# Stick-breaking attention: scores, transposes and value products in blocks of a unit, sigmoid written to SBUF, one ring of three PSUM bank pairs

## What is computed

```
z = q . k * scale                       strict: key index < query index
log_beta = log_sigmoid(z)
log_1mb  = where(strict, log_sigmoid(-z), 0)
later    = reverse_cumsum(log_1mb) - log_1mb
a        = where(strict, exp(log_beta + later), 0)
out      = a @ v, then a headwise RMSNorm
```

## Time and profile before

| | us |
|---|---|
| median of 3 runs | 2859.27 |
| profiled execution, its own time | 2860.66 |
| span of the profiled execution | 2858.8 |
| around the span | 1.9 |
| stick-breaking scans, first start | 915.4 |
| last difference, start | 1350.3 |
| first matmul of the output projection | 1364.9 |

### The profile page before, as it was taken

One profiled execution on the slowest core, in us unless ns is written; L12 is line 12 of the kernel. 1 busy time (PEld: TensorE's weight loads), 2 busy tenths in 40 slices (PEclk: granted clock), 3 DMA queues, 4 the chain that ended last, 5 costly groups with the idle time before them and its releaser, 6 DMA issues.

```text
span 2858.8 us, 51825 instructions
## 1 busy us (share of the span) xinstructions
PE 2788.6 (98%) x19192; PEld 2449.8 (86%) x19192; DVE 1894.1 (66%) x2800; ACT 1471.7 (51%) x2572; POOL 861.9 (30%) x947
## 2 busy tenths in 40 slices
PE   7999999999999999999999999999999999999998
PEld 6888778878888877777899999998889998999886
DVE  6214430087777777777577877787478877878656
ACT  5112221177777666666455545554355555655444
POOL 1832222066776786776002221111100000011110
PEclk9999999999999999999999999999999999999999
DMA  5489897466554523520559999999757784899984
GB/s 195 137 191 225 211 231 170 119 156 148 113 133 107 119 60 75 119 82 16 199 164 331 323 284 289 283 285 290 197 165 235 241 252 157 256 328 300 253 230 158
DMA packets 303337, 559.42 MB, mean 196 GB/s; under 512 B 32272, under 2 KB 70160, under 8 KB 301968
## 3 DMA queue, kind: packets, MB, share of 16 engines
q1 hardware_dynamic: 262768, 463.06, 51.0%
q0 software_dynamic: 39072, 92.30, 17.4%
q10 hardware_dynamic: 1312, 1.64, 0.2%
HBM read 449.91 MB, written 197.13 MB: 226 GB/s over the span
## 4 chain that ended last, share of the span: by engine, by line
PE 70%; DVE 4%; DMA 2%; ACT 2%; issue 1%; POOL 1%; SPq 0%; DVEq 0%; ACTq 0%; POOLq 0%
PE f_ps L2507 26%; PE f_ps L2391 19%; PE h_z L714 5%; PE h_o L1003 5%; PE h_z L717 5%; PE h_t L981 4%; PE h_o L939 3%; PE h_t L924 2%; DVE f_wlo L1880 1%; DMA f_wraw<-sums_scratch 1%; PE h_z L716 1%; DVE h_negmax L1178 1%; PE f_ps L2431 0%; PE f_ps L2417 0%; DVE f_xsum L2093 0%
## 5 line engine op out<-in xcount | busy, mean ns | idle before, releaser
L1880 DVE TENSOR_TENSOR f_wlo<-f_wraw,f_whi 128x512 fp32r<-128x512 f32 x834 | 574.7, 690 | 234.1 <-ACT f_whi L1873 232.3
L1873 ACT ACTIVATE f_whi<-f_wraw 128x512 fp32r<-128x512 f32 x834 | 520.8, 627 | 393.8 <-PE f_ps L2507 254.3
L2507 PE MATMUL f_ps<-f_hi_s,f_whi 128*128 128x256 f32 x1408 | 391.2, 278 | 7.1 <-DVE f_up L2232 7.1
L2507 PE MATMUL f_ps<-f_lo_s,f_whi 128*128 128x256 f32 x1408 | 391.7, 278 | 0.0
L2507 PE MATMUL f_ps<-f_hi_s,f_wlo 128*128 128x256 f32 x1408 | 389.8, 277 | 0.0
L1364 POOL TENSOR_TENSOR h_work<-h_more 128x1024 f32<-128x1024 f32 (+7 forms) x192 | 264.7, 1395 | 115.6 <-DVE h_more L1264 115.6
L2507 PE MATMUL f_ps<-f_hi_a,f_whi 128*128 128x256 f32 x1056 | 292.0, 276 | 1.0 <-DVE f_second L2232 1.0
L2507 PE MATMUL f_ps<-f_hi_a,f_wlo 128*128 128x256 f32 x1056 | 291.6, 276 | 0.0
L2507 PE MATMUL f_ps<-f_lo_a,f_whi 128*128 128x256 f32 x1056 | 291.6, 276 | 0.0
L2507 PEld LDWEIGHTS f_ps<-f_hi_s,f_whi 128*128 128x128 f32 x1408 | 264.4, 188 | 8.8 <-DVE f_wlo L1880 4.4
L1264 DVE TENSOR_TENSOR_SCAN h_more<-h_z,h_zero 128x1024 f32<-128x1024 f32 (+7 forms) x128 | 231.7, 1812 | 59.4 <-ACT h_z L1096 56.9
(11 more groups left out here) (203 smaller groups left out, 6448.2 us busy)
## 6 DMA issues: line engine op xcount, KB each, us to landing
f_wraw<-in_w_stream SPq DMA_DIRECT2D x394, 256.0 KB, 4.3
f_wraw<-sums_scratch SPq DMA_DIRECT2D x352, 256.0 KB, 4.8
sums_scratch<-in_w_stream POOLq DMA_DIRECT2D x132, 256.0 KB, 5.4
act_scratch<-f_act SPq DMA_DIRECT2D x88, 256.0 KB, 4.0
combined_acts<-f_act SPq DMA_DIRECT2D x88, 256.0 KB, 5.2
f_wraw<-down_sums SPq DMA_DIRECT2D x88, 256.0 KB, 3.5
f_piece<-combined_acts SPq DMA_DIRECT2D x88, 256.0 KB, 3.1
down_sums<-in_w_stream POOLq DMA_DIRECT2D x66, 256.0 KB, 6.3
```

Source lines behind the costliest of these rows:

```text
L1873: act.activation(w_hi[ring][:], w_raw[ring][:], ACT.Copy).then_inc(S["hi_split"], 1)
L1880: dve.tensor_tensor(w_lo[ring][:], w_raw[ring][:], w_hi[ring][:].bitcast(F32), ALU.subtract).then_inc(S["lo_split"], 1)
L2507: mm = pe.matmul(outs[i], w[ring][:, col], a[name][:, c, :], start=(c == 0 and m == 0), stop=(c == 3 and m == 2))
```

## The change

- PE's block i becomes: scores of both maps, transposes of both maps, then all value products of the piece (`stick_apply` has no halves any more). `lay` moves behind the transposes.
- `gate` writes the sigmoid to a new SBUF tile `gated[m]` and no longer back to PSUM; it waits for the scan of e - 2, which reads that tile. `scan` reads `gated[m]`. Scores no longer wait for a scan.
- `z[0]`, `z[1]` and `t_bank` become `ring[0..2]`. A table, built ahead, gives each score tile and each transposed tile the next of the three slots. Whoever takes a slot waits for its last holder: for the sigmoid where that was a score tile, for the evacuation where it was a transposed tile.
- ACT does gate, gate, evacuate, evacuate, and `settle` last.
- At the end the first transposes of the next stage (`ahead`) stand between the last two transposes of this one.
- To make room, `lambdas` and `lam_prod` lie in `squares`.

```diff
-        z = [memory.enter_context(nc.psum_tensor(f"h_z{s}", [P, CHUNK], F32)) for s in range(2)]
-        t_bank = memory.enter_context(nc.psum_tensor("h_t", [P, CHUNK], F32))
+        gated = [sb(f"h_gated{m}", [P, CHUNK]) for m in range(2)]
+        ring = [memory.enter_context(nc.psum_tensor(f"h_z{s}", [P, CHUNK], F32)) for s in range(3)]
...
+        scores_in, turned_in, held_by, place = {}, {}, [None, None, None], 0
+        for i in range(len(pieces) + 2):
+            for m in range(2):
+                if i < len(pieces):
+                    slot = m if i < 2 else place % 3
+                    scores_in[2 * i + m], held_by[slot] = (slot, held_by[slot]), ("gated", 2 * i + m + 1)
+                    place += i >= 2
+            for m in range(2):
+                if 0 <= i - 2:
+                    slot = place % 3 if i <= len(pieces) else 2
+                    turned_in[2 * (i - 2) + m], held_by[slot] = (slot, held_by[slot]), ("evacuated", 2 * (i - 2) + m + 1)
+                    place += 1
...
             def stick_scores(t, m):
-                if e < 2:
+                slot, holder = scores_in[e]
+                if holder is None:
                     pe.wait_ge(D["exped"], diff_steps)
                 else:
-                    pe.wait_ge(S["scanned"], e - 1)
-                score_matmuls(pe, z[m], query_of(s), k_st[s], m, t["segs"], (ident_bf, strict)).then_inc(S["scored"], 1)
+                    pe.wait_ge(S[holder[0]], holder[1])
+                score_matmuls(pe, ring[slot], query_of(s), k_st[s], m, t["segs"], (ident_bf, strict)).then_inc(S["scored"], 1)
...
             def breaking(i):
-                if cur is None and turning is None:
-                    pe.wait_ge(S["scanned"], len(sticks))
-                    ahead()
                 for m in range(2):
                     if cur is not None:
                         stick_scores(cur, m)
+                for m in range(2):
                     if turning is not None:
                         stick_turn(sticks[turning["steps"][m]])
-                    if applying is not None:
-                        stick_apply(applying, m)
-                    if m == 0 and closing is not None:
-                        lay(closing)
+                    if turning is pieces[-1] and m == 0:
+                        pe.wait_ge(S["evacuated"], len(sticks) - 2)
+                        ahead()
+                if closing is not None:
+                    lay(closing)
+                if applying is not None:
+                    stick_apply(applying)
...
             def gate(e):
-                act.activation(z[e % 2][:], z[e % 2][:], ACT.Sigmoid, scale=-1.0).then_inc(S["gated"], 1)
+                if e >= 2:
+                    act.wait_ge(S["scanned"], e - 1)
+                act.activation(gated[e % 2][:], ring[scores_in[e][0]][:], ACT.Sigmoid, scale=-1.0).then_inc(S["gated"], 1)
...
             def scan(e, t):
-                    done = dve.tensor_tensor_scan(buffer[:, a:b][:, ::-1], z[m][:, cols_of(seg)][:, ::-1],
+                    done = dve.tensor_tensor_scan(buffer[:, a:b][:, ::-1], gated[m][:, cols_of(seg)][:, ::-1],
                                                   zero[:].to_broadcast([P, seg["tiles"] * P]), begin, ALU.mult, ALU.add)
```

More of the change, by code:

```diff
@@ L966, in stick_scores, with stick_apply @@
                     pe.wait_ge(inner[s], 64 * use)
[L967 removed]
+                slot, holder = scores_in[e]
+                if holder is None:
                     pe.wait_ge(D["exped"], diff_steps)
                 else:
[L970 to L971 removed]
+                    pe.wait_ge(S[holder[0]], holder[1])
+                score_matmuls(pe, ring[slot], query_of(s), k_st[s], m, t["segs"], (ident_bf, strict)).then_inc(S["scored"], 1)
             def stick_turn(step):
                 e = step["e"]
+                slot, holder = turned_in[e]
                 pe.wait_ge(S["multiplied"], e + 1)
[L976 to L977 removed]
+                if holder is None:
+                    pe.wait_ge(D["evacuated"], diff_units)
                 else:
[L979 removed]
+                    pe.wait_ge(S[holder[0]], holder[1])
                 for j in range(CHUNK_TILES):
[L981 removed]
+                    mm = pe.transpose(ring[slot][:, j * P:(j + 1) * P], work[step["slot"]][:, j * P:(j + 1) * P], ident[:])
                 mm.then_inc(S["transposed"], 1)
[L984 removed]
+            def stick_apply(t):
                 s = t["p"] % 2
[L988 to L991, removed]
+                if t["r"] == 0 and t["c"] == 0:
+                    pe.wait_ge(values[s], 16 * (t["p"] // 2 + 1))
+                pe.wait_ge(S["evacuated"], t["steps"][1] + 1)
                 for seg in t["segs"]:
@@ L1006, in stick_apply @@
                                            stop=(seg["closes"] and j == seg["tiles"] - 1))
-                if half:
-                    mm.then_inc(S["applied"], 1)
+                mm.then_inc(S["applied"], 1)
             def lay(t):
@@ L1049, in exponential @@
                     total_of = row_sum[R["set"]][:, col:col + 1] if seg["two"] else both[R["set"]][:, col - 2:col - 1]
-                    done = act.activation(probs[R["set"]][k][:, cols_of(seg)], z[t["z"]][:, cols_of(seg)], ACT.Exp,
+                    done = act.activation(probs[R["set"]][k][:, cols_of(seg)], ring[t["z"]][:, cols_of(seg)], ACT.Exp,
                                           bias=neg_max[R["set"]][:, col:col + 1], accum_out=total_of)
@@ L1132, in breaking @@
                         gate(cur["steps"][m])
+                for m in range(2):
                     if turning is not None:
                         stick_evacuate(sticks[turning["steps"][m]])
-                    if m == 0 and closing is not None:
-                        settle(closing)
+                if closing is not None:
+                    settle(closing)
             if last_settle:
```

14 lines of the change are left out of this document (6 added, 8 removed).

## The result

The changed kernel takes 2994.57 us (median of 4 runs, 2990.64 to 2995.17), the one before 2864.49 us (median of 4, 2856.62 to 2872.22). The ratio is 1.0451, 95% interval 1.0416 to 1.0487: 4.5% slower. The forecast was 3003 us. The profiled execution took 2995.17 us, 134.5 more than that of before.

The account below looks back on a forecast made before the run. PE bounds the kernel before; in the changed stage DVE's scans and POOL's differences, taking turns, would. 2860.7 + 149 for the stretch - 6 at its end = 3004, median 1.4 under: 3003 us, range 2930 to 3090, chance 0.80.

Parts of the forecast that it names:

- Scans and differences on one time line: DVE's scan, now with two SBUF operands, and POOL's difference take turns by whole instructions: 317.7 + 264.7 = 582.4 us.
- Rival 2: Scan and difference share SBUF by the access, not the instruction: part of the loss, 2928 us, range 2850 to 2950; chance 0.05.
- the stretch: First scan to end of last difference: from 436.8 to 586 us, 149 us more, with +95 and +164 as ends.
- the normalizing: POOL's normalizing after a closed bank reads SBUF and holds DVE up: 34 us added, none to 42 possible.
- the turns' saving: A held-up scan or difference has 0.2 us of its start done when let go: 30 us off, ends 23 and 50.
- The upper end of the range: Top of the forecast's own range: 3025 us, up to 3060 if PE often drops to the lower clock and comes late.
- the order scan, scan, difference, difference: Order within a full piece, with two handovers; scans would average about 3.2 us, differences about 3.0.
- The end of the stage: Last difference to first projection matmul: from 12.65 to 6.7 us, 6 us less, since PE has caught up.
- PE's stalls: Idle weight loading before value products (L1003) and scores (L714) halves: 20.9 us off PE, counting for nothing under the time line.
- rival 1: The scan's broadcast zero column doesn't count as an SBUF operand, scans and differences still overlap, PE bounds: 2833 us; chance 0.12.
- Rival 3: PE falls to the lower clock and stays there: 3080 to 3150 us if half the time and more; chance 0.03.
- the slack of about 2 us a piece: PE needs 6.0 us of a full piece's 8.0 and waits for 2, mostly absorbing slower score blocks at the lower clock.

Follow-up runs that it names:

- e1: Kernel before, with only the sigmoid written to an SBUF tile and the scan reading it there; PE's and ACT's order and banks kept: 2992.97 us, ratio 1.0472.
- e2: e1 with the scan's other operand the score tile in PSUM (max for add), not the SBUF zero column; no longer stick-breaking: 2862.59 us, ratio 1.0008.
- e4: Changed kernel with the differences moved from POOL to DVE, behind both scans of a piece: 2904.9 us, 2 runs.
- e5: Changed kernel with POOL's differences replaced by a memset of the same tile, so POOL writes SBUF and reads nothing there: 2833.06 us, ratio 0.9919 to before.
- e6: Changed kernel with the normalizing's power replaced by a multiplication of the same elements, heads not normalized rightly: 2995.2 us, ratio 1.0451 to before.
- e7: Changed kernel with the first map's eight transposes of each piece done twice, more work for PE: 2997.88 us, ratio 1.0477 to before.
- e3: Kernel before with a new PE block order alone (both scores, first transposes, all value products, second transposes), sigmoid and scan in PSUM: 2847.65 us, ratio 0.9949.

## Why the prediction was right, point by point

**Scans and differences on one time line.** Right in mechanism, shown by e1, e2, e4 and e5, which each take away one other explanation. Rival 2, sharing by the access, is answered by the 64 scans that ended 2.14 or 2.15 us after the difference they began beside, however long they had been open. The sum's base, 317.7 + 264.7 = 582.4 us, was sound: the stretch took 573.9.

**The size: 586 us forecast, 573.9 measured.** The terms can be laid beside the trace, by adding up the starts and ends of its records from 914.89 to 1488.74 us. A scan or a difference is open (running or held up) for 548.9 us: 33.5 less than the 582.4, where the prediction took off 30. For the other 24.9 us neither is open. In them POOL multiplies for the norms (L1395 and L1369, 16.0 us) and takes their powers (L1391 and L1368, 6.7), DVE sums squares (2.3, partly beside these), and both engines are idle for 0.5 us. So the normalizing, put at 34 us, is the mis-sized term, by 9 us; the turns' saving adds 3.5. e6 bears this out from the other side: without the power the stage is 5 us shorter and not 23. Where a norm's instruction holds up a scan that is already open, its time lies in the 548.9, so the two terms can't be parted more finely than this. Both are within the bounds given. The prediction's "about 42 us in all" also leaves out another norm that POOL computes in this stretch (L1352 and L1353, 5.1 and 5.3 us before), which was in part made up by putting the rest too high.

**The total: 3003 us forecast, 2994.57 measured.** It is nearer than its main term by some luck: 12.5 us too many in the stretch were partly made up by 3.0 us behind the stage, where nothing was changed, and by an end of the stage that won 1 us less than forecast. The upper end of the range, 2860.7 + 164 = 3025, leaves out the 6 us of that end, which the lower end has.

**How the waiting shows: partly wrong.** I expected the order scan, scan, difference, difference, scans at 3.2 us and differences at 3.0, both engines over 90% busy. Scans came to 3.3, differences only to 2.2, the engines to 80% and 82% from 1000 to 1480 us. In the timeline scan and difference alternate one by one, so a scan is held up inside its record, while a difference mostly has not begun: it waits for its scan, and that shows as idle time (71 us of POOL's at the full shape). The two busy shares therefore hide a line that is all but full: a scan or a difference is open for 548.9 of 573.9 us. The sum hardly depends on the order.

**The end of the stage.** 6 us less forecast, 5.0 measured (12.65 to 7.7).

**PE's stalls.** Halved in number before value products as said (131 to 66); before scores they fell from 115 to 34, since PE now often waits there for a sigmoid instead. They are worth nothing in the changed kernel: e1, which keeps the old order of blocks and its 133 stalls, takes the same time (2992.97), and e7 adds work to PE for nothing. The prediction named the stalls before L1003 and L714 only; the largest group, 24.7 us before the mask's L716, it passed over, and since that one stays, nothing followed from it. Where nothing takes turns they are worth what the prediction put on them: 20.9 us and some small change forecast for rival 1, 27 measured in e5 and 15 in e3.

**Rival 3, the clock.** PE fell to the lower clock more often (15 times in the stage against once, a mean of 0.95 from 1000 to 1480 us) but did not stay there, and it cost nothing (e7): the slack of about 2 us a piece absorbs it, as the range's text had it.

Sum of the profiled execution: +137.1 for the stretch, -5.0 at its end, -0.6 for an earlier first scan, +3.0 behind the stage, where nothing was changed and 0.2% is noise: 134.5 us.

## What to carry to other kernels

Before moving an operand from PSUM to SBUF, count the SBUF operands of the DVE instruction, a broadcast column included, and look at whether POOL reads SBUF in the same stage: two engines that overlapped here at about 75% each became one line of 150%. In a trace such a pair is told by records of one form whose durations differ by up to about the length of the other engine's instruction: full scans spread from 2.3 to 3.9 us here, with differences of 1.9. And where PE bounds, grouping matmuls that load 64 columns apart from those that load 128 wins the stall of each change, if the chain behind still keeps pace; here that was 15 us of 2863 in e3.

## What the runs showed that I had not expected

- A POOL power of 128x8 elements, 1.64 us alone, lets a scan run beside it (e6), while a POOL multiplication of 512 columns does not: at 1108.11 us one of 1.04 us ran, and a scan of 256 columns begun at 1108.23 lasted 1.47 us, where 0.66 is its time alone.
- The 0.17 us stall stands at nearly every change between weights of 64 and of 128 columns, in either direction, and goes with the neighbours, not with the line: transposes behind scores hardly ever had one (once in the kernel before), and in e3, behind value products, they have it 66 times (12.6 us). No run changed the width of the weights alone, so that the width is the cause is likely but not shown.
- Moving POOL's work to an already busier DVE is cheaper than letting the two take turns: 2904.9 against 2994.57 us. The prediction had not considered it; the expectation of e4 had.
